# One chain step per unit, chain products on two banks, and retention folded into other bursts, in a two-layer hybrid decoder trunk

## The chip, the cores and the metric

The kernel runs on one core of one Trainium2 chip. The metric is the device time of one execution, in microseconds (us). The kernel before takes 576.5 us, the median of three runs (576.31 to 576.83).

## The reference

Two layers work on x, 512 tokens of width 1024, in float32. Each layer normalises x, projects it with one 1024 x 3904 matrix, sends the columns to four groups of width 256 (four heads of 64), multiplies each group's result by its SiLU gate, and adds the output projection of all four to x. Cut to what this change touches:

```python
def hybrid_layer(x, norm_w, w_in, w_out, ...):
    h = rmsnorm(x, norm_w)
    proj = h @ w_in
    p_rwkv, p_conv, p_moba, p_ret = jnp.split(proj, [...], axis=-1)
    y_rwkv = rwkv7_time_mix(p_rwkv[..., :RWKV_IN], ...) * jax.nn.silu(p_rwkv[..., RWKV_IN:])
    y_conv = short_conv_mix(p_conv[..., :3 * G], conv_w) * jax.nn.silu(p_conv[..., 3 * G:])
    y_moba = moba_attention(q, k, v, rel_bias) * jax.nn.silu(p_moba[..., 3 * G:])
    y_ret = retention_chunkwise(q, k, v) * jax.nn.silu(p_ret[..., 3 * G:])
    return x + jnp.concatenate([y_rwkv, y_conv, y_moba, y_ret], axis=-1) @ w_out

# rwkv7_time_mix, one step of the scan over tokens (then a layer norm per head)
state = (state * w_t[:, :, None, :] - s_kk[..., None] * (kk_t * a_t)[:, :, None, :]
         + v_t[..., None] * k_t[:, :, None, :])
y_t = jnp.einsum('bhij,bhj->bhi', state, r_t)

# retention_chunkwise, one step of the scan over chunks of 128 tokens
inner = jnp.einsum('bhnd,bhmd->bhnm', qc, kc) * decay_intra
y = jnp.einsum('bhnm,bhmd->bhnd', inner, vc) + jnp.einsum('bhnd,bhde->bhne', qc * q_decay, R)
R = R * chunk_decay + jnp.einsum('bhmd,bhme->bhde', kc * k_decay, vc)
# and after the scan: y = y * lax.rsqrt(mean(y * y) + NORM_EPS) per head
```

## The kernel before

**The stream of projections.** The large products are split in two parts each (`act_hi`, `act_lo`, `w_hi`, `w_lo`), and each of eight blocks of the inner dimension takes three matmuls of 128x512: one tile of the projection is 24 of them, in lines L772 to L775. The function `quarter` issues a quarter of a tile, 6 matmuls. A tile goes to PSUM bank 0 or 1 in turn. ScalarE makes `w_hi` (`tile_high`, L1295), GpSimd makes `w_lo` (L706), and ScalarE or VectorE takes the finished tile out of its bank (`copy`, L1403; the sigmoid or tanh of a gate, L1369; `conv_h`, L1479).

**The order.** Nothing is scheduled at run time. `layer_steps()` (L147 to L205) writes one list of steps, and every engine walks the same list and does its own part of each step. In the second half of a layer the list is built from 16 last tiles, retention's gates, attention's q and k, attention's gates, then the convolution's c, h, b and gates. Each tile has two slots of two quarters. `mid[i]` is what stands between the two quarters of slot i, `after[i]` what stands behind slot i: short bursts of small matmuls, and steps of ScalarE and VectorE only. An engine that has to wait in one step does not take the next.

**What hangs in the slots.**
- RWKV works on 8 chunks of 64 tokens: `inverse_x`, `inverse_y`, `corner_x`, `corner_t` build triangular inverses (they read `t_back`, data that went out to DRAM and come back transposed), `chunk_b` and `chunk_uw` the factors, `chunk_gh` what each chunk does to the state, then six steps `chain` 1 to 6 carry the state from chunk to chunk: TensorE (L1111 to L1124) multiplies, VectorE (L1938) scales, adds and stores the next state. `chunk_h`, `chunk_q`, `chunk_y1` and `chunk_y` make the outputs, `ln_square`, `ln_var`, `ln_recip` (L2009), `ln_scale` (L2014 on VectorE, L1541 on ScalarE) and `rwkv_finish` (L2018, L1867) the layer norm and the gate.
- Retention: `retain_scores`, `retain_state`, `retain_sum`, `retain_inner`, `retain_past`, `retain_out`, then its norm: `ret_low`, `ret_stat` (means on TensorE L885, added on VectorE L1984, L1987), `ret_root` (two square roots on ScalarE, L1560), `ret_recip` 0 to 3 (L1995), `ret_finish` 0 and 1 (L2002, L1867).
- Attention: six units (the loop over `u`), each `attend_scores` (TensorE L1008; VectorE adds the bias and takes the maximum, L1844, L1849; ScalarE the exponentials, L1464), `attend_norm` (L1856, L1859), `attend_turn` (transposes on TensorE L1019; ScalarE copies them out, L1470) and `attend_values` (L1035).

**Banks.** PSUM has eight banks. `bank_jobs()` (L225 to L320) lists for each job its bank and how many readers it has, in the order of the steps. `begin(job)` on TensorE waits until the previous user of that bank has been read by all its readers. Every chain step uses bank 7, and its four products of 64x64 stand side by side in it.

**The end of a layer.** The gate of the last tiles, `split_y` for each eighth of the concatenated y (ScalarE `act_hi`, L1572; VectorE `act_lo`, L2023) in the order `Y_ORDER`, and `out` 0 to 4, the output projection, which takes its blocks in that order.

## Time and profile before

| | |
|---|---|
| profiled execution, device time | 576.78 us |
| its span, first to last instruction | 575.0 us |
| TensorE matmul busy | 567.4 us, 99% of the span |
| VectorE, ScalarE, GpSimd busy | 381.0, 278.3, 249.3 us |
| mean granted TensorE clock | 0.997 |
| DMA, share of 16 engines' time, hardware queue | 39.4% |
| longest DMA groups: issue to landing | 3 to 8 us |

The span is 1.8 us shorter than the device time of the same execution; the profiled execution is 0.3 us above the median of the three runs. The first row of the table's engines is to be read with care: matmuls are pipelined, a 128x512 matmul is shown as 0.39 us long while the next starts 0.23 us after it, so "busy" says that TensorE had work in hand, not that every matmul came as early as it could. The granted clock is 0.9 of full speed or more in each fortieth of the span but the last (0.8).

### The profile page before, as it was taken

To read this page: it belongs to the slowest core of one execution; us is meant where nothing else is said; L and a number is where in the kernel's file an instruction comes from. 1 tells how busy PE (TensorE), PEld (TensorE's weight loads), DVE (VectorE), ACT (ScalarE), POOL (GpSimd) and SP (SyncE) were. 2 spreads that over 40 slices of the span, in tenths; PEclk is the share of its full clock that TensorE was granted. 3 is DMA by queue.
4 is the path that set the end of the run, shared out by engine and by line. 5 is a ranking of instruction groups with operands and counts; after the bars stand their busy time and mean duration, and the time that the engine had idled before them with its cause. 6 is when DMAs were issued, how large, how long until landed. Compare 5 with 4: busy or idle time off the path is not lost. (4 is left out here: it accounts for less than half of the span.)

```text
span 575.0 us, 12739 instructions
## 1 busy us (share of the span) xinstructions
PE 567.4 (99%) x5244; PEld 464.0 (81%) x5244; DVE 381.0 (66%) x644; ACT 278.3 (48%) x555; POOL 249.3 (43%) x197
## 2 busy tenths in 40 slices
PE   9999999999999999999999999999999999999995
PEld 7978888888877777888898788888888777788884
DVE  4999976482488557774543897947537865778163
ACT  5486231343574475534656743324357335735253
POOL 4946552044941323536335455402386313145340
PEclk9999999999999999999999999999999999999998
DMA  9546634056432122353535423332743321224513
GB/s 281 161 130 206 212 97 111 8 130 149 109 79 75 39 75 62 113 171 132 165 117 139 111 77 108 88 70 58 161 127 83 77 73 39 73 75 147 184 40 143
DMA packets 103373, 64.58 MB, mean 112 GB/s; under 512 B 29151, under 2 KB 94227, under 8 KB 103316
## 3 DMA queue, kind: packets, MB, share of 16 engines
q1 hardware_dynamic: 103316, 63.77, 39.4%
q8 instruction: 42, 0.69, 0.5%
q14 instruction: 15, 0.12, 0.1%
HBM read 55.61 MB, written 8.14 MB: 111 GB/s over the span
## 5 line engine op out<-in xcount | busy, mean ns | idle before, releaser
L706 POOL TENSOR_TENSOR w_lo<-w_raw,w_hi 128x512 fp32r<-128x512 f32 x156 | 216.6, 1409 | 283.0 <-ACT w_hi L1295 277.7
L772 PE MATMUL bank<-act_hi,w_hi 128*128 128x512 f32 x432 | 173.2, 401 | 0.0
L775 PE MATMUL bank<-act_lo,w_hi 128*128 128x512 f32 x432 | 168.5, 390 | 0.0
L774 PE MATMUL bank<-act_hi,w_lo 128*128 128x512 f32 x416 | 162.3, 390 | 0.0
L1295 ACT ACTIVATE w_hi<-w_raw 128x512 fp32r<-128x512 f32 x140 | 80.3, 622 | 74.1 <-PE bank L857 28.2
L772 PEld LDWEIGHTS bank<-act_hi,w_hi 128*128 128x128 f32 x432 | 81.1, 188 | 24.7 <-issue 8.2
L775 PEld LDWEIGHTS bank<-act_lo,w_hi 128*128 128x128 f32 x432 | 81.1, 188 | 17.4
L774 PEld LDWEIGHTS bank<-act_hi,w_lo 128*128 128x128 f32 x416 | 78.2, 188 | 14.8
L1221 PE MATMUL bank<-w_hi,act_hi 128*128 128x512 f32 x128 | 50.0, 390 | 0.0
L1223 PE MATMUL bank<-w_hi,act_lo 128*128 128x512 f32 x128 | 49.8, 389 | 0.0
L1222 PE MATMUL bank<-w_lo,act_hi 128*128 128x512 f32 x128 | 49.8, 389 | 0.0
L2028 DVE TENSOR_TENSOR x_or_y<-x_or_y,bank 128x512 f32<-128x512 f32 x16 | 11.0, 688 | 37.7 <-PE bank L1223 37.7
L1223 PEld LDWEIGHTS bank<-w_hi,act_lo 128*128 128x128 f32 x128 | 24.0, 188 | 5.1
L1222 PEld LDWEIGHTS bank<-w_lo,act_hi 128*128 128x128 f32 x128 | 24.0, 188 | 4.9
L1221 PEld LDWEIGHTS bank<-w_hi,act_hi 128*128 128x128 f32 x128 | 24.0, 188 | 4.9
L1464 ACT ACTIVATE pages<-pages,small 128x128 f32<-128x128 f32 (+3 forms) x32 | 17.9, 561 | 19.0 <-DVE small L1849 19.0
L855 PE MATMUL bank<-w_hi,act_hi 128*128 128x512 f32 x64 | 25.5, 398 | 0.0
L857 PE MATMUL bank<-w_hi,act_lo 128*128 128x512 f32 x64 | 25.0, 390 | 0.0
L856 PE MATMUL bank<-w_lo,act_hi 128*128 128x512 f32 x64 | 24.9, 390 | 0.0
L1369 ACT ACTIVATE x_or_y<-bank 128x512 f32<-128x512 f32 x16 | 9.6, 599 | 30.1 <-PE bank L775 30.1
L1470 ACT ACTIVATE pages<-bank 128x384 f32<-128x384 f32 (+1 forms) x24 | 11.4, 527 | 26.4 <-PE bank L1019 26.3
L1403 ACT ACTIVATE pages<-bank 128x512 f32<-128x512 f32 x16 | 9.6, 600 | 28.5 <-PE bank L775 28.5
(217 smaller groups left out, 961.0 us busy)
## 6 DMA issues: line engine op xcount, KB each, us to landing
w_raw<-in_w_in_dram SPq DMA_DIRECT2D x62, 512.0 KB, 4.1
w_raw<-in_w_out_dram SPq DMA_DIRECT2D x16, 512.0 KB, 3.8
pages<-in_x_dram SPq DMA_DIRECT2D x4, 512.0 KB, 6.3
x_or_y<-in_x_dram SPq DMA_DIRECT2D x4, 512.0 KB, 4.2
x_scratch<-x_or_y SPq DMA_DIRECT2D x4, 512.0 KB, 2.9
x_or_y<-x_scratch SPq DMA_DIRECT2D x4, 512.0 KB, 3.7
out_dram<-pages SPq DMA_DIRECT2D x8, 256.0 KB, 2.2
bias_scratch<-pages SPq DMA_DIRECT2D x1, 1280.0 KB, 8.1
```

The source lines that it names most:

```text
L706: ins = pool.tensor_tensor(low, raw, w_hi[:, i % HI, k, 0:n].bitcast(F32), ALU.subtract)
L772: mm(b[:, :], hi, act_hi[:, k, :], start=n == 0, stop=False)
L774: mm(b[:, :], lo, act_hi[:, k, :], start=False, stop=False)
L775: ins = mm(b[:, :], hi, act_lo[:, k, :], start=False, stop=n == KT - 1)
L855: mm(o, act_hi[:, n, tc], w_hi[:, :, n, :], start=n == 0, stop=False)
L856: mm(o, act_hi[:, n, tc], w_lo[:, :, n, :], start=False, stop=False)
L857: ins = mm(o, act_lo[:, n, tc], w_hi[:, :, n, :], start=False, stop=n == KT - 1)
L1221: mm(b[:, :], act_hi[:, k, tc], hi[:, wc], start=first, stop=False)
L1222: mm(b[:, :], act_hi[:, k, tc], lo[:, wc], start=False, stop=False)
L1223: ins = mm(b[:, :], act_lo[:, k, tc], hi[:, wc], start=False, stop=last)
L1295: go(w_hi[:, i % HI, k, 0:n], w_raw[:, i % RAW, k, 0:n], ACT.Copy).then_inc(s("w_high"), 1)
L1464: go(pb, pb, ACT.Exp, bias=row_max[:, n:n + 1], accum_out=row_sum[:, n:n + 1]).then_inc(s("prob"), 1)
```

## The change

- **Prologue.** The seven idle matmuls before the first projection become one, and VectorE waits for the norm weights' banks where it first reads them.
- **Retention.** `retain_scores` moves forward, behind RWKV's `scores` 2 and 3, into banks 2 and 3; `rotate rk1` and `wide 0 0` go ahead of those two steps. `retain_state` joins `chunk_b` in `after[1]`, `retain_inner` joins `inverse_x`, `retain_past` and `retain_out` 0 join `corner_x`, `retain_out` 1 `corner_t`. `ret_low`, `ret_stat`, `ret_root` and the first `ret_recip` come one to two slots later.
- **Chain.** Each attention unit u carries one chain step u+1 in `after[12+2u]`; before, steps stood in every slot or second slot from 13 on. All of attention moves one slot later. A chain step now writes two banks: 7, and the bank of the tile before the one that has just been computed (`1 - place_of[...]`). Its four products lie in four different 64x64 quarters of the array (the "quarter tiles"). VectorE stores the state with three instructions instead of two, and copies the first state and the chunk-end decays with three instead of one.
- **Layer norm.** `chunk_y1` comes in two halves, `chunk_y` moves from `after[19]` to `after[24]`, `ln_square` from `mid[21]` to `mid[25]`, `ln_var` from `mid[22]` to `after[26]`, and the four `ln_recip` from slots 22 to 26 to slots 26 to 28.
- **Output.** `Y_ORDER` ends 2, 3, 0, 1 instead of 0, 1, 2, 3 (0 and 1 are RWKV's eighths), and both `rwkv_finish` come later.

The diff, with parts left out:

```diff
@@ -147,8 +147,8 @@
...
-          ("copy", "rk0"), ("rotate", "rq1"), ("scores", 0), ("scores", 1), ("copy", "rk1"), ("rotate", "rk0"), ("to_rows", "v"), ("scores", 2),
-          ("scores", 3), ("wide", 0, 0), ("wide", 0, 1), ("rotate", "rk1"), ("wide", 0, 2), ("wide", 0, 3),
+          ("copy", "rk0"), ("rotate", "rq1"), ("scores", 0), ("scores", 1), ("copy", "rk1"), ("rotate", "rk0"), ("to_rows", "v"), ("rotate", "rk1"), ("wide", 0, 0), ("scores", 2),
+          ("scores", 3), ("retain_scores",), ("wide", 0, 1), ("wide", 0, 2), ("wide", 0, 3),
...
@@ -159,40 +159,39 @@
...
-    after[0] += [("retain_state",), ("retain_scores",)]
-    after[1] += [("retain_sum",), ("inverse_eye",)]
-    after[2] += [("retain_inner",), ("chunk_b",)]
...
-                    (INV0 + 2, ("corner_x",)), (INV0 + 3, ("corner_t",)), (9, ("ret_stat",)), (10, ("chunk_uw",)),
-                    (11, ("chunk_gh",)), (17, ("chunk_y1",)), (21, ("ln_square",)), (22, ("ln_var",))]:
...
+    after[1] += [("retain_state",), ("chunk_b",), ("inverse_eye",)]
+    after[2] += [("retain_sum",)]
+    after[9] += [("ret_low",)]
+    mid[10] += [("ret_stat",)]
+    for i, step in [(INV0, ("inverse_x",)), (INV0, ("retain_inner",)),
+                    (INV0 + 1, ("inverse_y",)), (INV0 + 1, ("inverse_yt",)),
+                    (INV0 + 2, ("corner_x",)), (INV0 + 2, ("retain_past",)), (INV0 + 2, ("retain_out", 0)),
+                    (INV0 + 3, ("corner_t",)), (INV0 + 3, ("retain_out", 1)), (10, ("chunk_uw",)),
...
-    after[9] += [("ret_root",), ("ret_recip", 0)]
+    after[10] += [("ret_root",), ("ret_recip", 0)]
...
-            mid[11 + 2 * u].append(("attend_turn", u - 1))
-            after[11 + 2 * u].append(("attend_values", u - 1))
...
-        if u in (1, 2, 3):
-            after[11 + 2 * u].append(("chain", 2 * u))
+                after[12 + 2 * u].append(("attend_out", u // 3 - 1))
         if u < UNITS:
-            (after[11 + 2 * u] if u else mid[10]).append(("attend_scores", u))
-            (mid[12 + 2 * u] if u else after[11]).append(("attend_norm", u))
-    mid[15][1:1] = [("chunk_q",), ("queries",)]
...
+            after[12 + 2 * u].append(("chain", u + 1))
+            (after[12 + 2 * u] if u else mid[11]).append(("attend_scores", u))
+            (mid[13 + 2 * u] if u else after[11]).append(("attend_norm", u))
+    after[12].append(("chunk_h",))
+    after[14].append(("chunk_q",))
+    mid[15].append(("queries",))
+    after[16].append(("chunk_y1", 0))
...
+    after[24].append(("chunk_y",))
+    after[26].append(("ln_var",))
+    for i, step in [(12, ("ret_recip", 1)), (16, ("ret_recip", 2)), (18, ("ret_recip", 3)), (19, ("ret_finish", 0)), (20, ("ret_finish", 1)),
+                    (21, ("conv_taps", 0)), (24, ("conv_taps", 1)), (26, ("ln_recip", 0)), (26, ("ln_recip", 1)), (27, ("ln_recip", 2)), (28, ("ln_recip", 3)),
+                    (27, ("ln_scale", 0)), (28, ("ln_scale", 1))]:
         after[i].append(step)
...
-    s += [("split_y", k) for k in Y_ORDER[:4]] + [("rwkv_finish", 1), ("split_y", 0), last[-1], ("conv_out", 0), ("split_y", 1), ("conv_out", 1)]
+    s += [("split_y", k) for k in Y_ORDER[:4]] + [("rwkv_finish", 0), last[-1], ("conv_out", 0), ("conv_out", 1), ("split_y", 2), ("split_y", 3), ("rwkv_finish", 1)]
...
-Y_ORDER = [6, 7, 4, 5, 0, 1, 2, 3]
-ROW_ORDER = [3, 2, 0, 1]
+Y_ORDER = [6, 7, 4, 5, 2, 3, 0, 1]
+ROW_ORDER = [3, 2, 1, 0]
...
         elif kind == "chain":
-            layer.append((f"chain{step[1]}", 7, 1))
+            layer += [(f"chain{step[1]}_0", 7, 1), (f"chain{step[1]}_1", 1 - place_of[projections[-1]], 1)]
         elif kind == "retain_scores":
-            layer += [("rs0", 5, 1), ("rs1", 6, 1)]
+            layer += [("rs0", 2, 1), ("rs1", 3, 1)]
...
-            idle(3)
             pe.wait_ge(s("const_a"), 16)
             turn(0, 0)
             turn(1, 0)
-            idle(4)
+            idle(1)
...
+                    banks = [begin(f"chain{c}_{p}", layer) for p in range(2)]
                     for p in range(2):
                         for hh in range(2):
-                            r = slice(64 * hh, 64 * hh + 64)
-                            ins = mm(b[r, p * N:(p + 1) * N], GT[r, p, c, :], ST[r, p, c, :], start=True, stop=True)
-                    end(ins, f"chain{c}", layer)
+                            r = head_rows(hh)
+                            ins = mm(banks[p][head_rows(hh ^ p), 0:N], GT[r, p, c, :], ST[r, p, c, :], start=True, stop=True)
+                        end(ins, f"chain{c}_{p}", layer)
...
-                        mark(dve.tensor_copy(w_end[:].rearrange("p a c -> p (a c)").unsqueeze(2), flat[:, :, CH:CH + 1]))
+                        mark(dve.tensor_copy(w_end[:, 0, :].unsqueeze(2), flat[:, 0:NCH, CH:CH + 1]))
+                        for hh in range(2):
+                            mark(dve.tensor_copy(w_end[head_rows(1 - hh), 1, :].unsqueeze(2), flat[head_rows(hh), NCH:2 * NCH, CH:CH + 1]))
...
-                    dve.tensor_copy(ST[:, :, 1, :], HP[:, :, 0, :]).then_inc(s("first_state"), 1)
+                    dve.tensor_copy(ST[:, 0, 1, :], HP[:, 0, 0, :]).then_inc(s("first_state"), 1)
+                    for hh in range(2):
+                        dve.tensor_copy(ST[head_rows(hh), 1, 1, :], HP[head_rows(1 - hh), 1, 0, :]).then_inc(s("first_state"), 1)
...
+                    b = [ps(f"chain{c}_{p}", layer) for p in range(2)]
+                    stt(ST[:, 0, c + 1, :], b[0][:, 0:N], w_end[:, 0, c:c + 1], HP[:, 0, c, :], ALU.mult, ALU.add).then_inc(done(f"chain{c}_0", layer), 1)
+                    for hh in range(2):
+                        o = head_rows(1 - hh)
+                        ins = stt(ST[head_rows(hh), 1, c + 1, :], b[1][o, 0:N], w_end[o, 1, c:c + 1], HP[o, 1, c, :], ALU.mult, ALU.add)
+                    ins.then_inc(done(f"chain{c}_1", layer), 1)
```

ScalarE's order around the exponentials of unit 0 and the copy of the tile `mk1` (the last row), in the first layer, before (L1560 is `ret_root`, L1498 `chunk_uw`, L1295 `tile_high`, L1464 the exponentials, L1403 the copy):

```order
L1560 ACTIVATE pages<-pages 128x512 [waits bank3_read]
L1498 ACTIVATE pages<-bank 128x512 [waits bank7_full]
L1498 ACTIVATE pages<-bank 128x512 [waits bank5_full]
L1498 ACTIVATE pages<-bank 128x512 [waits bank6_full]
L1498 ACTIVATE pages<-bank 128x512 [waits bank4_full]
L1295 ACTIVATE w_hi<-w_raw 128x512 [waits w_loaded1,bank0_full] x2
L1464 ACT_TABLE_LOAD
L1464 ACTIVATE pages,small<-pages,small 128x128 [waits logit_max]
L1464 ACTIVATE pages,small<-pages,small 128x256 [waits logit_max]
L1464 ACTIVATE pages,small<-pages,small 128x128 [waits logit_max]
L1464 ACTIVATE pages,small<-pages,small 128x256 [waits logit_max]
L1403 ACTIVATE pages<-bank 128x512 [waits bank1_full]
```

and now (the same functions stand two lines further down):

```order
L1500 ACTIVATE pages<-bank 128x512 [waits bank4_full]
L1297 ACTIVATE w_hi<-w_raw 128x512 [waits w_loaded1,bank0_full] x2
L1562 ACT_TABLE_LOAD
L1562 ACTIVATE pages<-pages 128x512 [waits bank2_read]
L1562 ACTIVATE pages<-pages 128x512 [waits bank3_read]
L1466 ACT_TABLE_LOAD
L1466 ACTIVATE pages,small<-pages,small 128x128 [waits logit_max]
L1466 ACTIVATE pages,small<-pages,small 128x256 [waits logit_max]
L1466 ACTIVATE pages,small<-pages,small 128x128 [waits logit_max]
L1466 ACTIVATE pages,small<-pages,small 128x256 [waits logit_max]
L1405 ACTIVATE pages<-bank 128x512 [waits bank1_full]
```

The square roots and their table load stood ahead of the four copies of `chunk_uw`; now they stand behind them and behind `tile_high`, next to the exponentials. The copy of `mk1` follows the exponentials in both.

VectorE's order at the same place, from the first `ret_recip` on, before (L1995 `ret_recip`, L1844 and L1849 `attend_scores` 0, L1911, L1904 and L1916 `chunk_gh`):

```order
L1995 RECIPROCAL pages<-pages 128x256 [waits ret_root]
L1844 SCALAR_TENSOR_TENSOR pages<-bank,bias 128x128 [waits bank2_full,bias_back]
L1844 SCALAR_TENSOR_TENSOR pages<-bank,bias 128x256
L1849 TENSOR_REDUCE small<-pages 128x1 [waits bank2_read]
L1849 TENSOR_REDUCE small<-pages 128x1
L1844 SCALAR_TENSOR_TENSOR pages<-bank,bias 128x128 [waits bank3_full]
L1844 SCALAR_TENSOR_TENSOR pages<-bank,bias 128x256
L1849 TENSOR_REDUCE small<-pages 128x1 [waits bank3_read]
L1849 TENSOR_REDUCE small<-pages 128x1
L1995 RECIPROCAL pages<-pages 128x256 [waits ret_root]
L1911 TENSOR_TENSOR pages<-bank,constants 128x4x64 [waits bank5_full]
L1911 TENSOR_TENSOR pages<-bank,constants 128x4x64
```

and now:

```order
L2004 RECIPROCAL pages<-pages 128x256 [waits ret_root]
L1915 TENSOR_TENSOR pages<-bank,constants 128x4x64 [waits bank5_full]
L1915 TENSOR_TENSOR pages<-bank,constants 128x4x64
L1915 TENSOR_TENSOR pages<-bank,constants 128x4x64 [waits bank6_full]
L1915 TENSOR_TENSOR pages<-bank,constants 128x4x64
L1908 TENSOR_TENSOR pages<-bank,chunk_decay 128x64 [waits bank7_full]
L1908 TENSOR_TENSOR pages<-bank,chunk_decay 128x64
L1908 TENSOR_TENSOR pages<-bank,chunk_decay 128x64 [waits bank4_full]
L1908 TENSOR_TENSOR pages<-bank,chunk_decay 128x64
L1920 COPY pages<-pages 128x64 [waits bank4_read,bank7_read]
L1922 COPY pages<-pages 64x64 x2
L1848 SCALAR_TENSOR_TENSOR pages<-bank,bias 128x128 [waits bank2_full,bias_back]
```

Unit 0's scores, which `logit_max` waits for, stood directly behind the first reciprocal; now `chunk_gh` with eleven instructions stands between.

VectorE's order at the end of the layer, before (L2009 `ln_recip`, L1888 `conv_b`, L2014 `ln_scale`, L2018 and L1867 `rwkv_finish`, L1777 a gate, L2023 `split_y`):

```order
L2009 RECIPROCAL pages<-pages 128x256 [waits bank7_read]
L1884 SCALAR_TENSOR_TENSOR pages<-pages,params 128x512 [waits conv_tap]
L1884 SCALAR_TENSOR_TENSOR pages<-pages,params 128x512 [waits dve_step]
L1888 TENSOR_TENSOR pages<-pages,bank 128x512 [waits bank0_full,dve_step]
L2009 RECIPROCAL pages<-pages 128x256 [waits bank5_read] x2
L2014 TENSOR_TENSOR pages<-pages 128x512 [waits dve_step]
L1888 TENSOR_TENSOR pages<-pages,bank 128x512 [waits bank1_full]
L2014 TENSOR_TENSOR pages<-pages 128x512 [waits dve_step]
L2018 TENSOR_TENSOR pages<-pages 128x512 [waits ln_affine]
L1867 SCALAR_TENSOR_TENSOR x_or_y<-pages,x_or_y 128x512 [waits dve_step]
L1777 SCALAR_TENSOR_TENSOR x_or_y<-x_or_y,bank 128x512 [waits bank0_read]
L2023 TENSOR_TENSOR act_lo<-x_or_y,act_hi 128x512 [waits y_hi] x4
```

and now:

```order
L1892 TENSOR_TENSOR pages<-pages,bank 128x512 [waits bank0_full]
L2018 RECIPROCAL pages<-pages 128x256 [waits bank7_read] x2
L1892 TENSOR_TENSOR pages<-pages,bank 128x512 [waits bank1_full]
L2018 RECIPROCAL pages<-pages 128x256 [waits bank5_read]
L2023 TENSOR_TENSOR pages<-pages 128x512 [waits dve_step]
L2018 RECIPROCAL pages<-pages 128x256 [waits bank5_read]
L2023 TENSOR_TENSOR pages<-pages 128x512 [waits dve_step]
L1781 SCALAR_TENSOR_TENSOR x_or_y<-x_or_y,bank 128x512 [waits bank0_read]
L2032 TENSOR_TENSOR act_lo<-x_or_y,act_hi 128x512 [waits y_hi] x4
```

All four reciprocals now stand behind the first `conv_b`, two of them behind the second or directly ahead of it, and `rwkv_finish` 0 has gone from ahead of the gate and the first splits to behind them.

## Rows read from the trace of the kernel before

**Rows 1.** Waits of TensorE over the span: us in total, times, longest.

```profile
PE bank L740 <- POOL pages L680: 1.0, 1, 1.0
PE bank L1035 <- ACT pages L1470: 0.3, 2, 0.2
PE bank L1047 <- issue: 0.2, 1, 0.2
```

**Rows 2.** Timeline of TensorE, slots 10 and 11 of layer 0: start, duration, line.

```profile
159.18 1.98 PE L1063 MATMUL bank<-pages 64*64 64x128 f32 x64
160.98 0.83 PE L1008 MATMUL bank<-pages 64*64 64x128 f32 x16
161.74 0.50 PE L772 MATMUL bank<-act_hi,w_hi 128*128 128x512 f32 x1
...
164.68 1.16 PE L1099 MATMUL bank<-pages 64*64 64x64 f32 x64
...
166.34 0.50 PE L772 MATMUL bank<-act_hi,w_hi 128*128 128x512 f32 x1
```

**Rows 3.** Timeline of ScalarE, the same slots.

```profile
159.84 1.15 ACT L1560 ACTIVATE pages<-pages 128x512 f32<-128x512 f32 x2
160.90 2.04 ACT L1498 ACTIVATE pages<-bank 128x512 f32<-128x512 f32 x4
162.81 1.17 ACT L1295 ACTIVATE w_hi<-w_raw 128x512 fp32r<-128x512 f32 x2
...
166.58 0.49 ACT L1464 ACTIVATE pages<-pages,small 128x256 f32<-128x256 f32 x1
...
168.05 0.60 ACT L1403 ACTIVATE pages<-bank 128x512 f32<-128x512 f32 x1 [0.89 <-PE bank L775]
```

**Rows 4.** Timeline of VectorE, the same slots.

```profile
160.50 1.75 DVE L1995 RECIPROCAL pages<-pages 128x256 f32<-128x256 f32 x1 [1.71 <-ACT pages L1560]
162.17 0.56 DVE L1844 SCALAR_TENSOR_TENSOR pages<-bank,bias 128x128 f32<-128x128 f32 x2
...
164.47 1.74 DVE L1995 RECIPROCAL pages<-pages 128x256 f32<-128x256 f32 x1
166.13 1.35 DVE L1911 TENSOR_TENSOR pages<-bank,constants 128x256 f32<-128x256 f32 x4
167.40 0.61 DVE L1904 TENSOR_TENSOR pages<-bank,chunk_decay 128x64 f32<-128x64 f32 x4
```

**Rows 5.** Timeline of VectorE, unit 2: its first score and last norm.

```profile
178.14 0.56 DVE L1844 SCALAR_TENSOR_TENSOR pages<-bank,bias 128x384 f32<-128x384 f32 x1 [0.15 <-PE bank L1008]
...
182.30 0.42 DVE L1859 TENSOR_SCALAR pages<-pages,small 128x384 f32<-128x384 f32 x1
```

**Rows 6.** Timeline of VectorE, norms of unit 0, two pairs.

```profile
168.44 0.55 DVE L1859 TENSOR_SCALAR pages<-pages,small 128x128 f32<-128x128 f32 x2
...
169.10 1.64 DVE L1859 TENSOR_SCALAR pages<-pages,small 128x128 f32<-128x128 f32 x2
```

**Rows 7.** Timeline of GpSimd, the same microseconds.

```profile
169.31 2.59 POOL L706 TENSOR_TENSOR w_lo<-w_raw,w_hi 128x512 fp32r<-128x512 f32 x2 [3.19 <-ACT w_hi L1295]
```

**Rows 8.** Timeline of ScalarE, end of layer 0.

```profile
238.35 1.28 ACT L1369 ACT_TABLE_LOAD   x1
241.63 0.60 ACT L1369 ACTIVATE x_or_y<-bank 128x512 f32<-128x512 f32 x1 [1.99 <-PE bank L775]
```

**Rows 9.** Timeline of VectorE, end of layer 0.

```profile
236.80 0.69 DVE L2014 TENSOR_TENSOR pages<-pages 128x512 f32<-128x512 f32 x1
...
243.82 3.82 DVE L2023 TENSOR_TENSOR act_lo<-x_or_y,act_hi 128x512 fp32r<-128x512 f32 x4 [0.87 <-ACT act_hi L1572]
```

**Rows 10.** Timeline of TensorE, `inverse_x` of layer 0.

```profile
138.29 1.16 PE L944 MATMUL bank<-pages 64*64 64x64 f32 x64
```

**Rows 11.** Timeline of SyncE's queue, the loads of `t_back`, layer 0.

```profile
129.37 2.66 SPq L526 DMA_DIRECT2D pages<-t_scratch  x4
```

**Rows 12.** Timeline of TensorE, the idle matmuls ahead of the first projection.

```profile
11.56 1.25 PE L740 MATMUL bank<-pages 128*128 128x128 f32 x8
```

54 lines of the change are left out of this document (23 added, 31 removed).

## Prediction

> A difference below 0.2% (1.2 us) can't be told from no change in this kernel. I forecast **585.5 us**, 1.6% slower.
>
> **What bounds the kernel now.** I read the shares first: TensorE has work in hand for 99% of the span. Then its waits: beside one microsecond at the very start, the whole execution holds 0.3 us behind the copies of turned probabilities and 0.2 us without a cause that the profile shows [rows 1]. So every microsecond counts that TensorE's stream gains or loses, and the other engines count only where they make it wait. Then I read the timelines of slots 10 to 12 side by side, since the change packs reciprocals, chunk results, scores and the first chain step there [rows 2 to 4]. In them the 12 matmuls between two bursts take 164.68 - 161.74 = 2.94 us, where 12 in an undisturbed run take 12 x 0.227 = 2.72 [rows 2]. Last the end of the layer [rows 8, 9]: the tanh of the second-last gate at 241.63 waits for its tile, not for the norm; the tile of the last gate follows it, 24 x 0.227 = 5.4 us, so `out` 0 starts about E = 246.9.
>
> **The main term: chain step 1 waits for a bank.** Times here count from the start of `chunk_uw`.
> TensorE now runs `chunk_uw` (160.98 - 159.18 = 1.8), 12 matmuls (2.9), `chunk_gh` (166.34 - 164.68 = 1.7) with unit 0's scores (161.74 - 160.98 = 0.8), 18 matmuls (one and a half times 2.94, less a slow start: 4.3), and stands before chain 1 at 11.5 [rows 2]. That step writes bank 7 and the bank of `mk1`, so it waits until ScalarE has copied `mk1`.
> That copy stands behind the four exponentials of unit 0. ScalarE: the copies of `chunk_uw` end near 3.1, one after the last product is there (2.04 long from 1.0), `tile_high` 1.17 -> 4.2, table load 1.28 [rows 8] -> 5.5, square roots 1.15 for both, the first at 6.1 [rows 3]. VectorE: reciprocal 1.75 less the overlap of neighbours -> 7.8; four additions of `chunk_gh` 1.35 -> 9.1; decays 0.61 -> 9.7; three small copies, where there was one, about 0.5 (an estimate from the decays, 0.15 each) -> 10.2; scores and maxima of unit 0 as between 162.17 and 164.47, 2.3 -> 12.5 [rows 4]. ScalarE: the last exponential 0.49 and its read-out -> 13.2, the copy 0.60 -> 13.9 [rows 3]. The wait is 13.9 - 11.5 = 2.4 us a layer. Now that row at 168.05 waits 0.89 for its own tile, and nothing waits for it.
> Bounds: if every operation of VectorE overlaps as well as its neighbours there, 1.8; if its adds meet GpSimd's halves (below), 3.4. I take 2.4, for both layers 4.8.
>
> **Turn 4 waits for its norm.** VectorE has, behind unit 4's scores, the second `ret_finish`, a chain step of three instructions and then the reciprocals and norms. The nearest case, unit 2, has the first score at 178.14 and the last norm ending at 182.72 [rows 5], with `ret_finish` between: 4.6 us. TensorE comes after 18 matmuls, 4.3. That alone makes 0.3. What is added is GpSimd. A pair of norms takes 0.55 us, the next pair 1.64: it starts at 169.10, GpSimd's subtraction at 169.31, and the pair ends at 170.74, just after the first of the two (half of 2.59) [rows 6, 7]. ScalarE makes `w_hi` behind a tile's end, and GpSimd starts 0.8 us later, which is where unit 4's norm falls. I take 1.2; bounds 0.25 (norm clear of GpSimd) and 2.2 (both norms caught). Turns 2 and 3 have no `ret_finish` ahead and pass by about 0.2 us: 0.1 together. Two layers: 2.6.
> The Trainium skill, "SBUF — State Buffer", on engine ports, describes this as an exclusive lock between VectorE and GpSimd that is held for the full instruction; the trace agrees with its 1.64 against 0.55.
>
> **Values 4 and 5.** Before the copies of the turned probabilities ScalarE now has the copy of a `conv_h` tile, which waits for VectorE. Such a copy is 0.6 long [rows 3]; those waits are the 0.3 in two places now [rows 1]. I take 0.35 for each unit, 0.7 a layer, between 0 and 1.2; two layers 1.4.
>
> **`out` 0 waits for the splits.** `ln_var` has moved from `mid[22]` to `after[26]`, 5 slots before E: 5 x 2.7 and the run-in behind bursts, E - 14.5. Its burst and the square roots (1.15 for two [rows 3]) end at E - 13.1. VectorE then has, in this order, two reciprocals (1.7 each: E - 9.8), `conv_b` 1 (0.6), the third reciprocal (E - 7.4), `ln_scale` 0 (0.6), the fourth (E - 5.0), `ln_scale` 1 (E - 4.3). ScalarE scales behind that (0.8: E - 3.5), loads the tanh table (1.28 [rows 8]: E - 2.2) and only then does the tanh of gate 0. From that tanh to the first four splits' first end is 3.1 us now: tanh at 241.63, first split at 243.82 and 0.9 of its 3.82 for four [rows 8, 9]. So E - 2.15 + 3.1 = E + 0.95, where TensorE is ready at E. Now it is E - 2.1. I take 1.0; bounds 0 and 2.0 (an `ln_recip` or split caught by GpSimd). Two layers 2.0. `rwkv_finish` 0 no longer stands ahead of the gate on VectorE; without that move the wait would be longer by its two instructions.
>
> **What TensorE gains.** By the list, the second half of a layer has 21 separate bursts instead of 22: `retain_scores` rides in an existing stretch, and `retain_state` joins `chunk_b`. A burst less saves the slow start (2.94 against 12 x 0.227 = 2.72) and the drain behind its last record, 0.35. The count of small matmuls stays. With the few tenths of smoother runs and today's waits [rows 1] I take 0.7 a layer, between 0.2 and 1.2; two layers -1.4. The four products of a chain step in four quarters change nothing in my sum: by `inverse_x`'s 64 records in 1.16 us [rows 10] the eight records of a step take 0.15, 0.3 with a drain.
> The Trainium skill, "TensorEngine Tiling (Array Packing)", Key Properties, says that different tiles load and multiply in parallel. If that halved each step, the gain would be at most 0.15 x 12 = 1.8 and the time 583.7; no row here shows it, and I don't count it.
>
> **Once only.** `inverse_x` comes 2.9 us earlier than its 138.29 [rows 10], at 135.4: the four loads of `t_back` are issued until 129.37 + 2.66 = 132.0 and need some 3.4 more to land [rows 11], 135.4. Level: I take +0.3, bounds 0 and 0.8. The wait of `chunk_b` without a cause [rows 1] may go or move: -0.2. The idle matmuls ahead of the first projection take 1.0 of 1.25 us for four [rows 12]; three fewer are 0.75, of which the splits of the weights let about half through: -0.4, with bounds -0.75 and +1.0, since the clock granted there may rise later if TensorE did less before.
> Hidden: the two more copies of `w_end` (0.1 us on VectorE, with two microseconds to spare), a third instruction in each chain step, and `scores` 2 and 3 a little later.
>
> **Sum.** 4.8 + 2.6 + 1.4 + 2.0 - 1.4 + 0.3 - 0.2 - 0.4 = +9.1 us. On the profiled execution (576.8) that makes 585.9, on the median (576.5) 585.6. With all lower bounds: 3.6 + 0.5 + 0 + 0 - 2.4 - 0.2 - 0.75 = +0.8; with all upper ones over 15. Neither is likely, since the terms are independent.
>
> **Rivals.**
> - *TensorE's own work stays the bound* (the other side). Decisive is whether `mk1` is copied before 11.5: if exponentials or scores start 2.4 us earlier than I add up (the square roots done right behind the first copies of `chunk_uw`, or `chunk_gh` much shorter in its new place), the bank is free. With norms clear of GpSimd only the gains stay: -1.4 -0.6 = 574.5. For it: TensorE waits almost nowhere now. Against: ScalarE's list fixes the order, and each duration is a row.
> - *Only the bank's wait.* Chain 1 waits, but turn 4, the values and `out` are covered within tenths: 4.8 + 2 x 0.3 (turn 4 without GpSimd) - 1.4 - 0.3 = +3.7, 580.2. For it: those three margins are each below 1 us of my own adding up.
> - *GpSimd catches more.* Turns 2 and 3, 0.2 us from the edge, lose 1.2 each as well (4.8 over both layers; half of it, if one in two is caught, 2.4), and the prologue costs 1.0 instead of giving 0.4: 9.1 + 2.4 + 1.4 = +12.9, 589.4. For it: with all norms in the same place behind a tile's end, what happens in one unit happens in all.
>
> **Chances.** My forecast 0.5, only the bank 0.2, GpSimd more 0.2, TensorE's own work 0.1. The range from 578.5 to 591 leaves out the last rival and half a tenth above. Faster by over 0.2%: 0.09; within 0.2%: 0.05 (lower bounds throughout); slower: 0.86. The forecast's own range is 583 to 588.
>
> **What would show it.** In the profile after: a wait of TensorE at the chain's line in unit 0, ended by ScalarE's copy, 2 to 3 us, once in each layer; a wait at the turn of unit 4 ended by VectorE, with a norm over 0.8 us long beside GpSimd; a wait at the first matmul of `out` ended by the splits; no wait at `chunk_b`. If the copy of `mk1` ends before TensorE reaches the chain, the main term is wrong; if TensorE's waits sum to less than 3 us and the time is still above 580, the cost is in the stream itself.

## The result and the profile after

The changed kernel takes 600.2 us (median of four runs, 598.9 to 601.1) against 576.6 of the kernel before: ratio 1.041 (95% interval 1.038 to 1.043), 23.6 us slower. The forecast was 585.5 with a range up to 591. The direction was right; the loss was 2.6 times the forecast one (23.6 us for 9.1).

The profiled execution took 598.87 us with a span of 597.1, 22.1 us more than before. First the shares of the page:

```profile
PE 570.4 (96%) x5232; PEld 463.6 (78%) x5232; DVE 384.2 (64%) x664; ACT 277.5 (46%) x555; POOL 246.5 (41%) x197
```

TensorE's share fell from 99% to 96%, and its busy time still grew by 3.0 us, though it multiplies the same things. The waits of TensorE over the span (total, times, longest) answer to [rows 1]:

```profile
PE bank L1018 <- DVE pages L1863: 8.3, 6, 2.1
PE bank L1123 <- ACT pages L1405: 5.4, 2, 2.7
PE bank L1223 <- issue: 1.6, 2, 0.8
PE bank L1223 <- POOL w_lo L706: 1.5, 2, 0.8
PE bank L1034 <- ACT pages L1472: 1.2, 4, 0.4
PE bank L740 <- POOL pages L680: 1.0, 1, 1.0
PE bank L979 <- issue: 0.7, 1, 0.7
PE bank L734 <- DVE pages L1655: 0.5, 1, 0.5
PE bank L817 <- DVE act_lo L1645: 0.2, 1, 0.2
PE bank L817 <- POOL w_lo L706: 0.2, 1, 0.2
```

They add to 20.6 us where they were 1.5. So 19.1 of the 22.1 us are waits, and 3.0 lie outside them. Each is looked for in a timeline below.

**Chain step 1.** The place of [rows 2 to 4], now. TensorE (start, duration, operation; in brackets the wait and what ended it):

```profile
158.11 1.98 PE L1062 MATMUL bank<-pages 64*64 64x128 f32 x64
...
172.39 0.49 PE L1123 MATMUL bank<-pages 64*64 64x64 f32 x8 [2.69 <-ACT pages L1405]
172.63 0.48 PE L1102 MATMUL bank<-pages 64*64 64x64 f32 x6
...
175.58 0.50 PE L771 MATMUL bank<-act_hi,w_hi 128*128 128x512 f32 x1
```

ScalarE:

```profile
163.65 1.15 ACT L1562 ACTIVATE pages<-pages 128x512 f32<-128x512 f32 x2
...
169.61 0.40 ACT L1466 ACTIVATE pages<-pages,small 128x128 f32<-128x128 f32 x1 [3.50 <-DVE small L1853]
...
171.67 0.57 ACT L1405 ACTIVATE pages<-bank 128x512 f32<-128x512 f32 x1
```

VectorE:

```profile
164.31 1.75 DVE L2004 RECIPROCAL pages<-pages 128x256 f32<-128x256 f32 x1 [3.88 <-ACT pages L1562]
165.99 1.35 DVE L1915 TENSOR_TENSOR pages<-bank,constants 128x256 f32<-128x256 f32 x4
...
168.63 0.62 DVE L1848 SCALAR_TENSOR_TENSOR pages<-bank,bias 128x128 f32<-128x128 f32 x2
```

The step starts 14.3 us after the start of `chunk_uw` at 158.11, where the forecast had 13.9, and TensorE had been ready at 11.6 (forecast 11.5). ScalarE's order is what was forecast: square roots at 163.65 behind `tile_high`, exponentials from 169.61, the copy of `mk1` (L1405) at 171.67. The wait is 2.69 us; 2.4 was forecast.

Behind it stands what no term of the forecast held. Windows of three microseconds in the same trace (busy of each engine, then the granted TensorE clock, the DMA share and GB/s): ahead of the wait, behind it, and behind a later wait of 2.06 us:

```profile
166.00:169.00 3.00, 3.00 (x15) 2.46 (x14) 2.80 (x14) 0.10 (x1) 0.00 (x0) 1.00 0.59 166
172.40:175.40 3.00, 3.00 (x104) 3.00 (x104) 1.00 (x4) 0.89 (x2) 2.49 (x2) 0.50 0.00 0
211.00:214.00 3.00, 3.00 (x37) 2.09 (x36) 1.04 (x2) 0.49 (x1) 0.00 (x0) 1.00 0.66 174
```

The granted clock is 0.50 behind the chain's wait, 1.2 GHz instead of 2.4; the low stretch is 3.4 us long and begins in the last tenths of the wait. In it runs `chunk_h`, 96 short records: from 172.63 to the next full matmul at 175.58 is 2.95 us. In a1_bank4 (below), where this place runs at full clock, the same stretch takes 172.54 - 170.78 = 1.76. That is 1.2 us, and 1.0 in layer 1 (2.78 us). With the chain step itself it is 2.3 us for both layers: from chain step 1 to step 2 it is 10.33 and 10.18 us here, and 9.11 in each layer of a1.

**Unit 3 and unit 4.** VectorE around the norms (L1863) of unit 3 and unit 4:

```profile
205.79 1.74 DVE L2004 RECIPROCAL pages<-pages 128x256 f32<-128x256 f32 x1
...
207.59 0.55 DVE L1863 TENSOR_SCALAR pages<-pages,small 128x128 f32<-128x128 f32 x2
...
208.25 2.50 DVE L1863 TENSOR_SCALAR pages<-pages,small 128x128 f32<-128x128 f32 x2
...
217.05 0.68 DVE L2011 TENSOR_TENSOR pages<-pages 128x512 f32<-128x512 f32 x1
...
218.56 1.45 DVE L1863 TENSOR_SCALAR pages<-pages,small 128x384 f32<-128x384 f32 x1
...
220.13 1.23 DVE L1863 TENSOR_SCALAR pages<-pages,small 128x384 f32<-128x384 f32 x1
```

GpSimd in the same microseconds:

```profile
208.12 2.49 POOL L706 TENSOR_TENSOR w_lo<-w_raw,w_hi 128x512 fp32r<-128x512 f32 x2 [7.01 <-ACT w_hi L1297]
218.54 2.60 POOL L706 TENSOR_TENSOR w_lo<-w_raw,w_hi 128x512 fp32r<-128x512 f32 x2 [7.93 <-ACT w_hi L1297]
```

Between unit 3's scores and its norms stands `ret_recip` 3, the 1.74 us at 205.79. The first pair of norms takes 0.55 us; the second starts inside GpSimd's subtraction and takes 2.50. TensorE's turn of unit 3 waits 2.06 us for it. In unit 4 it is `ret_finish` 1 (L2011 and the line behind it, 1.3 us) that comes ahead of the norms, and both are caught: 1.45 and 1.23 us where 0.42 was [rows 5]. TensorE waits 1.29 and 0.79 us. Both layers show the same to a hundredth, which makes 8.3 us. The turns cost somewhat more than these waits: from chain step 4 to step 6, where both turns lie, it is 22.64 us in each layer, and 17.77 in a2_recip (below), which has none of the three waits. That is 9.7 us for both layers.

Unit 2 has a reciprocal ahead of its norms as well (`ret_recip` 2, 1.74 us at 195.84). There the last norm starts at 198.23 and GpSimd's subtraction at 198.28; the norm takes 0.49 us, and TensorE does not wait. So turn 2 passed by a few hundredths: the reciprocal costs time only where it pushes a norm into a subtraction.

**The output projection.** TensorE's two waits in it, in layer 0:

```profile
255.82 0.47 PE L1223 MATMUL bank<-w_hi,act_hi 128*128 128x512 f32 x1 [0.78 <-issue]
...
286.70 0.50 PE L1223 MATMUL bank<-w_hi,act_hi 128*128 128x512 f32 x1 [0.68 <-POOL w_lo L706]
```

The first, at its start, is the splits of the first y blocks (the profile names no releaser); 1.0 was forecast, 0.8 came. The second, 31 us later, waits for a `w_lo` of the output weights. No step of the forecast had it. SyncE's queue shows where it comes from (start, time to issue):

```profile
257.44 11.09 SPq L526 DMA_DIRECT2D x_or_y<-in_x_dram  x4
268.57 11.20 SPq L548 DMA_DIRECT2D w_raw<-in_w_out_dram  x4
```

The last of the four loads of x waits until the last y block is split (VectorE ends it at 268.17), and the next four weight tiles stand behind them in the queue: they start 268.57 - 255.82 = 12.8 us after the output projection does. In the kernel before, the same loads began 8.6 us after it, at 255.44, with the projection starting at 246.87, and the last split had ended at 255.04.

### The profile page after: what moved, and what is told of

The parts are those of the page before. It is cut to its first block, busy times and chain, and to the rows that moved or that the text cites. A ratio compares the mean times of both kernels' runs of the same rounds, so it can differ in the third digit from the quotient of the medians.

```text
span 597.1 us, 12755 instructions
## 1 busy us (share of the span) xinstructions
PE 570.4 (96%) x5232; PEld 463.6 (78%) x5232; DVE 384.2 (64%) x664; ACT 277.5 (46%) x555; POOL 246.5 (41%) x197
## 4 chain that ended last, share of the span: by engine, by line
PE 68%; DVE 15%; ACT 5%; DMA 4%; issue 3%; POOL 3%; SPq 0%; POOLq 0%; ACTq 0%; DVEq 0%
PE bank L771 13%; PE bank L774 13%; PE bank L773 12%; DMA w_raw<-in_w_out_dram 3%; POOL w_lo L706 3%; PE bank L854 3%; PE bank L856 2%; PE bank L855 2%; DVE act_lo L2032 2%; DVE pages L2018 2%; PE bank L1034 2%; PE bank L1223 2%; DVE pages L1848 2%; PE bank L1225 2%; PE bank L1224 2%
## 5 line engine op out<-in xcount | busy, mean ns | idle before, releaser
L706 POOL TENSOR_TENSOR w_lo<-w_raw,w_hi 128x512 fp32r<-128x512 f32 x156 | 213.9, 1391 | 304.1 <-ACT w_hi L1297 302.6
L773 PE MATMUL bank<-act_hi,w_lo 128*128 128x512 f32 x416 | 162.2, 390 | 0.0
L773 PEld LDWEIGHTS bank<-act_hi,w_lo 128*128 128x128 f32 x416 | 78.2, 188 | 15.0
L701 POOL TENSOR_TENSOR w_hi<-w_raw,units 128x512 fp32r<-128x512 f32 (+1 forms) x20 | 20.9, 1043 | 9.9 <-DMA w_raw<-in_w_in_dram 5.9
L1711 DVE TENSOR_TENSOR stat_lo<-pages,stat_hi 128x512 fp32r<-128x512 f32 x16 | 14.6, 933 | 14.7 <-ACT pages L1533 11.4
```

The source lines that it names most:

```text
L701: pool.tensor_tensor(w_hi[:, i % HI, k, 0:n], raw, one.unsqueeze(2).to_broadcast([P, H, n]), ALU.mult).then_inc(s("w_high_pool"), 1)
L706: ins = pool.tensor_tensor(low, raw, w_hi[:, i % HI, k, 0:n].bitcast(F32), ALU.subtract)
L773: mm(b[:, :], lo, act_hi[:, k, :], start=False, stop=False)
```

## The experiments

Thirteen kernels ran, in four groups; each group ran beside the kernel before on one chip (whose median was 576.5 to 577.0). Differences of about 1 us are read from the ratios.

**a1_bank4: the chain's second bank.**

```diff
-  (f"chain{step[1]}_1", 1 - place_of[projections[-1]], 1)
+  (f"chain{step[1]}_1", 4 if step[1] == 1 else 1 - place_of[projections[-1]], 1)
```

> The changed kernel with one bank moved: the second product pair of chain step 1 goes to bank 4 (free since first_state) instead of the bank of mk1. Theory W (each wait of TensorE is lost time, and the 2.7 us wait also halves the granted clock for 3.3 us behind it, in which chunk_h's 96 records take 2.95 instead of 1.65 us): both the wait (2 x 2.7) and the slow stretch (2 x 1.4) go, 600.2 - 8.2 = 592.0. Rival M (the wait moves: the norm of unit 0 or chain 2 is next): at most a third of it comes back, 597 or more, with a new wait at the first turn. Rival N (wait without clock effect): 5.4 come back, 594.8, and chunk_h still takes about 2.9 us.

Measured: 593.1 us (592.3 to 593.8), ratio 1.028 (1.026 to 1.030), 7.1 us less. No wait at the chain is left, and the stretch behind it is at full clock, so the wait was the bank's alone. But the slow clock has moved:

```profile
209.50:212.50 3.00, 3.00 (x30) 1.67 (x28) 0.23 (x1) 0.00 (x0) 0.00 (x0) 0.51 0.45 134
```

The same wait of 2.06 us at unit 3's turn (it ends at 207.78 here) is now followed by the half clock, which in the changed kernel it was not. Theory W was right on the stretch behind the chain and wrong that nothing would take its place: the trace has two slow stretches, as many as the changed kernel's. So between the two profiled executions only the waits came back: the spans differ by 5.5 us, the waits by 5.8. How often the clock falls is not fixed even within one kernel. The mean granted clock of a1's four executions is 0.991, 0.996, 0.994 and 0.994, the first one being the trace, and a slow stretch of 3.4 us takes 0.003 off that mean. This is where the medians' 7.1 us can hold more than the traces' 5.5.

**a4_idle: work in place of the wait.** The output of the ten matmuls is read by nobody.

```diff
                         pe.wait_ge(*at("first_state", layer))
+                        for _ in range(10):
+                            mm(bank[4][:, 0:P], ident, ident, start=True, stop=True)
```

> The changed kernel with ten more matmuls of 128x128 on constants, into bank 4, whose output nobody reads, between the wait for first_state and the wait for the banks in chain step 1. They fill some 2.5 of the 2.7 us in which TensorE waits. If the idle time drops the granted clock: the clock stays at 2.4 GHz, chunk_h takes 1.65 us again, 600.2 - 2.8 = 597.4. If the clock falls for another reason (the 64x64 shapes, the other engines' load): no change, 600.2, and chunk_h at 2.9 us.

Measured: 598.2 us (596.9 to 599.0), ratio 1.037 (1.035 to 1.039), 2.0 us less. The matmuls run from 169.26, the step starts at 172.11, no later than without them:

```profile
169.26 2.39 PE L1117 MATMUL bank<-constants 128*128 128x128 f32 x20
172.11 0.34 PE L1125 MATMUL bank<-pages 64*64 64x64 f32 x8 [0.46 <-ACT pages L1407]
```

The stretch behind the step is at full clock, and the clock falls behind the next long wait instead:

```profile
172.20:175.20 3.00, 3.00 (x109) 2.76 (x110) 2.04 (x9) 0.81 (x2) 2.52 (x2) 1.00 0.03 5
210.30:213.30 3.00, 3.00 (x16) 1.84 (x15) 0.21 (x1) 0.02 (x1) 0.00 (x0) 0.50 0.63 168
```

So the short shapes alone do not lower the clock; with the idle time filled, this place stays at full clock in both layers. Between the profiled executions nothing was won: the spans are 597.0 and 597.1, and two slow stretches stand at unit 3 in place of the two at the chain. The medians' 2.0 us fit the other executions, two of which have a mean granted clock of 0.996 where the changed kernel's four have 0.990 to 0.993.

**a2_recip: two steps of VectorE.**

```diff
-  (18, ("ret_recip", 3)), (19, ("ret_finish", 0)), (20, ("ret_finish", 1)),
+  (17, ("ret_recip", 3)), (19, ("ret_finish", 0)), (19, ("ret_finish", 1)),
```

> The changed kernel with two steps of VectorE moved: ret_recip 3 from after[18] to after[17], ret_finish 1 from after[20] to after[19]. Theory W: the reciprocal between unit 3's scores and norms pushes the norms into GpSimd's subtraction (one pair takes 2.50 us), and ret_finish does so for unit 4 (1.45 and 1.23 us). Without them the norms end before GpSimd starts: waits of 2.06 and 1.29 + 0.79 go in each layer, -8.3, 591.9. Rival M: the norms stay slow since GpSimd's start follows the same tile end, and only the 1.7 and 1.4 us of the moved steps count where they are longer than the margin: -3 to -4, 596.5.

Measured: 588.8 us (588.4 to 590.4), ratio 1.022 (1.020 to 1.024), 11.4 us less. TensorE's waits at the turns fall from 8.3 to 0.3 us:

```profile
PE bank L1123 <- ACT pages L1405: 5.4, 2, 2.7
...
PE bank L1018 <- DVE pages L1863: 0.3, 2, 0.2
```

Two steps that had idle time of VectorE half a slot or a slot ahead of them cost almost half of the whole change. Theory W had the 8.3. Of the further 3 us, 1.5 are what the turns cost beside their waits (9.7 in all), and a part is the slow clock: in this trace it comes in layer 0 only, though the chain's wait of 2.7 us is there in both layers.

**c2_bank_recip: both.** Edit: the two above together, without the idle matmuls.

> The changed kernel with both edits that gave time back: bank 4 for chain step 1, and ret_recip 3 and ret_finish 1 one slot earlier. In the two kernels with one edit each the stretch at half clock was still there, behind the wait that was left (behind unit 3's turn, or behind chain step 1). Theory W (a wait of 2 us or more can drop the clock, and no such wait is left): no stretch below full clock before the tail, and the gains add to more than their sum: 600.2 - 7.1 - 11.4 = 581.7 by the sum, about 580 with the last stretch gone. Rival (the clock falls for some other reason): a half-clock stretch of 3.3 us is still there in each layer, 582 or more.

Measured: 582.5 us (580.9 to 583.0), ratio 1.011 (1.009 to 1.012), 17.6 us less than the changed kernel. There is no stretch below full clock before the tail, over 568 us:

```profile
2.00:570.00 568.00, 562.45 (x5217) 458.89 (x5216) 377.52 (x657) 272.67 (x547) 246.97 (x188) 1.00 0.40 112
```

The longest wait left, but for the first microsecond, is 0.8 us. The single gains are 18.5 together, so the two add to a little less than their sum, not more, and the expected 580 was not reached.

**a3_ln: the layer norm one slot earlier.**

```diff
-  after[24].append(("chunk_y",)); after[26].append(("ln_var",)); (25, ("ln_square",))
+  after[23].append(("chunk_y",)); after[25].append(("ln_var",)); (24, ("ln_square",))
```

with the four `ln_recip` and two `ln_scale` one slot earlier as well (lines put together here).

> The changed kernel with the layer norm one slot earlier: chunk_y after[23], ln_square mid[24], ln_var after[25], the reciprocals and scales one slot earlier each. Theory W: VectorE's and ScalarE's chain ends 2.7 us earlier, out 0 finds its splits (-0.8), the last splits end 1.9 us earlier, with them the loads of x and of the next weights of the output projection, and the second wait in out (0.7) shrinks to 0.1 or less: -1.4 a layer, 597.4. Rival: the earlier chunk_y waits for chain 6 or meets GpSimd, and the gain is below 1 us (599.2 or more). A rival on the second wait: it comes from the one load fewer that was issued ahead of the norm weights, not from the splits; then only 0.8 a layer comes back, 598.6.

Measured: 605.1 us (604.4 to 606.6), ratio 1.050 (1.048 to 1.052), 4.9 us slower than the changed kernel. The edit was badly placed. `ln_square` in `mid[24]` stands ahead of unit 5's turn, and ScalarE works its list in order:

```profile
231.40 1.20 ACT L1510 ACTIVATE pages<-bank 128x512 f32<-128x512 f32 x2
232.68 0.63 ACT L1551 ACTIVATE stat_hi<-pages 128x512 fp32r<-128x512 f32 x1
233.21 0.61 ACT L1552 ACTIVATE pages<-pages 128x512 f32<-128x512 f32 x1
...
234.89 1.08 ACT L1472 ACTIVATE pages<-bank 128x512 f32<-128x512 f32 x2
```

Six instructions of the output's copies and squares (L1510 to L1552, 3.5 us) go ahead of the copies of the turned probabilities (L1472), and TensorE waits 2.65 us for those in each layer, with the half clock behind (in this trace the chain's wait has it in layer 0 only). The wait at the output's start did halve, 0.8 to 0.4.

**c3_bank_recip_ln: the same, with `ln_square` in `after[24]`, on top of c2.**

> As c2_bank_recip, and the layer norm one slot earlier, with ln_square behind unit 5's values (after[24]) instead of ahead of its turn, where ScalarE's squares held up the copies of the turned probabilities for 2.7 us. Theory W: out 0 waits 0 instead of 0.8 and the second wait in out falls below 0.2 instead of 0.5 to 0.8, as VectorE's last splits come earlier: -2.5 against c2, 577.5. Rival (the second wait hangs on the order of loads): -1.6, 578.5.

Measured: 581.4 us (580.1 to 582.5), ratio 1.008 (1.007 to 1.010), 1.1 us less than c2, which the intervals do not separate. The start of the output waits 0.4 instead of 0.8, but the wait at `w_lo` is 0.9 in each layer, no smaller, and the weight loads start 12.8 us behind the output's start as in c2 and in the changed kernel. So a norm one slot earlier does not cure that one.

**c4_old_end: c3 with the old order at the end.**

```diff
-Y_ORDER = [6, 7, 4, 5, 2, 3, 0, 1]
+Y_ORDER = [6, 7, 4, 5, 0, 1, 2, 3]
-... + [("rwkv_finish", 0), last[-1], ("conv_out", 0), ("conv_out", 1), ("split_y", 2), ("split_y", 3), ("rwkv_finish", 1)]
+... + [("rwkv_finish", 1), ("split_y", 0), last[-1], ("conv_out", 0), ("split_y", 1), ("conv_out", 1)]
```

and `rwkv_finish` 0 back in `after[28]`, `ROW_ORDER` as before.

> As c3_bank_recip_ln, with the old order at the end (Y_ORDER, ROW_ORDER and the places of rwkv_finish as before). Theory E: the wait at w_lo (0.9 a layer) goes, since the last splits and the loads behind them come earlier; but rwkv_finish 0 stands ahead of the gate on VectorE again and lengthens the wait at out 0 from 0.4 to about 1.5: 581.4 - 1.8 + 2.2 = 581.8. Rival W: the w_lo wait stays and out 0 waits longer: 583.5.

Measured: 579.7 us (579.4 to 580.1), ratio 1.005 (1.003 to 1.006), 1.7 us less than c3 (1.9 by the ratios). The `w_lo` wait is gone, the weight loads start 11.1 us behind the output's start, and the start of the output waits no longer than in c3:

```profile
PE bank L1035 <- ACT pages L1473: 1.9, 4, 0.7
...
PE bank L1224 <- issue: 0.8, 2, 0.4
```

I had expected `rwkv_finish` 0 on the way to the gate to cost 1.1 us a layer there; it stands in time in which VectorE waited for ScalarE anyway.

**b6_end: the end's order alone, on the kernel before.** Edit: the reverse of the last one.

> The kernel before with the end's part of the change alone: the y blocks in the order 6, 7, 4, 5, 2, 3, 0, 1, rwkv_finish 0 behind the first four splits, rwkv_finish 1 and the splits of 0 and 1 last; the layer norm where it was. Theory E (the second wait in out, 0.7 us a layer, comes from this order: the last splits end 12.4 us after the output projection starts instead of 8.5, and the loads of x and of the next weights stand behind them on SyncE): a wait of 0.4 to 0.8 in each layer at a w_lo, +1.2, 577.7, and no wait at out 0. Rival W (it comes from the later layer norm alone): no new wait, 576.5.

Measured: ratio 1.000 (0.999 to 1.001), and no new wait. The order at the end costs nothing where the norm stands as in the kernel before: the first splits start 3.1 us ahead of the output there, in c3 only 1.0, and the weight loads 10.1 us behind its start. So c4 shows that the wait needs the new order, and b6 that the order alone does not bring it. That the late norm is the other half fits these times; it was not tried alone with the old order.

**b2_two_banks: the chain's two banks and quarters alone, on the kernel before.** Edit: the hunks of the diff on `chain`, `first_state` and `w_end`, and in `by_chunk` the place of "h"; every step stays in its slot.

> The kernel before with the chain's part of the change alone: two banks, four products in four 64x64 quarters, three instructions of VectorE to a step instead of two, three copies of the first state and of w_end; all steps in their old places. Theory W: the chain stands beside covered work on VectorE: between 0 and +0.6, 576.8. Rival Q (products in different quarters run side by side): 0.15 us less for each of 12 steps, 574.7. Rival V (VectorE's third instruction reaches the turns behind it): +0.3 us for each of 12 steps, 580.

Measured: 580.0 us (579.6 to 581.6), ratio 1.006 (1.005 to 1.007), 3.4 us slower. The expectations missed the reason:

```profile
PE bank L773 <- DVE pages L1948: 3.8, 6, 0.8
```

L773 is the first matmul of a new tile. Chain steps 2, 4 and 6 stood in the odd `after` there, between two tiles, and the bank they borrow is the one in which the next tile starts at once: it waits 0.8, 0.4 and 0.8 us for VectorE to read the product. In the changed kernel the steps stand in the even `after`, in the middle of a tile, and that wait does not exist. Two more waits, 0.6 and 0.4 us, are of the "issue" kind (below). The step itself did get shorter. The first chain step and the record behind it, in the kernel before:

```profile
172.04 0.45 PE L1123 MATMUL bank<-pages 64*64 64x64 f32 x8
172.33 0.33 PE L1103 MATMUL bank<-pages 64*64 64x64 f32 x6
```

and in b2:

```profile
173.39 0.34 PE L1125 MATMUL bank<-pages 64*64 64x64 f32 x8
173.56 0.33 PE L1104 MATMUL bank<-pages 64*64 64x64 f32 x6
```

The next record comes 0.28 or 0.29 us behind a step's first one before, and 0.16 or 0.17 in b2, in all twelve steps. That is 0.12 us a step, 1.4 in all, near Rival Q's 0.15; the new waits hide it in the time. The two banks and the four quarters came together, so the rows do not tell which of them it is.

**b1_retention and b5_ret_past: retention's part alone, on the kernel before.**

```diff
-  after[0] += [("retain_state",), ("retain_scores",)];  after[2] += [("retain_inner",), ("chunk_b",)]
+  after[1] += [("retain_state",), ("chunk_b",), ("inverse_eye",)]; after[2] += [("retain_sum",)]
   # both: retain_scores behind scores 3, retain_inner with inverse_x
   # b1:   retain_past, retain_out 0 with inverse_y (mid[6]), retain_out 1 mid[7], ret_low after[7], ret_stat mid[9]
   # b5:   retain_past, retain_out 0 with corner_x (mid[7]), retain_out 1 mid[8], ret_low after[8], ret_stat after[9]
```

> The kernel before with retention's part of the change alone: retain_scores behind scores 3 in banks 2 and 3, retain_state with chunk_b, retain_inner with inverse_x, retain_past and retain_out 0 with inverse_y, retain_out 1 with corner_x; the norm of retention stays where it was. Theory W: one burst fewer in each layer, 0.35 each, and the wait in chunk_b gone: -0.7 to -1.0, 575.6. Rival (inverse_x comes too early for its transposed data and waits, retain_out 1 too late for ret_low): +0.5 to +1.5, 577.5.

> As b1_retention (the kernel before with retention folded into other bursts), but retain_past and retain_out 0 stand with corner_x as in the changed kernel, and retention's means follow one half slot later, in after[9]. In b1 the only new waits were 0.98 and 1.41 us inside retain_past, which the profile puts down to nothing, where three bursts of 64 short matmuls follow each other (inverse_y, inverse_yt, retain_past). Theory F (a third burst in a row runs out of instructions): with two in a row there is no such wait, b1 - 2.4 = 576.0, and against before -0.5. Rival (retain_past waits for its data, which retain_sum makes late): the wait moves along or is gone by the later place, but the means then wait: 577 or more.

Measured: b1 578.4 us, ratio 1.003 (1.002 to 1.004), slower; b5 576.2 us, ratio 0.999 (0.998 to 1.000), a shade faster. In b1 TensorE stops inside `retain_past` (L1190), the third burst in a row:

```profile
141.36 1.16 PE L979 MATMUL bank<-x_or_y,pages 64*64 64x64 f32 x64
142.34 1.13 PE L990 MATMUL bank<-pages,x_or_y 64*64 64x64 f32 x64
143.27 0.43 PE L1190 MATMUL bank<-pages 64*64 64x64 f32 x8
144.68 1.03 PE L1190 MATMUL bank<-pages 64*64 64x64 f32 x48 [0.98 <-issue]
```

Eight records have run when it stops, so it does not wait for the burst's first data, and the profile names no releaser ("issue"). With two bursts in a row b5 has no such wait, nor any other but the first microsecond of the span. That fits TensorE running out of instructions, and the traces hold a sign of it. The profile has a DMA queue that it calls "instruction", which moves 42 blocks of 16 KB in each execution. b1's transfers from 142.1 to 142.4 us hold one, which starts at 142.21, 2.5 us ahead of the restart at 144.68:

```profile
q8 instruction: 1, 0.02, 24.4%
```

The fifteen traces, with those of the two kernels compared, hold 15 such stops apart from the waits at the output projection's start; each ends 2.3 to 3.1 us behind the start of such a block, and 1.3 to 1.7 us behind its end. I call the cause likely: the times agree in each case, and b5 takes the stop away, but no run changed the supply of instructions alone. The changed kernel had the same kind of wait once, 0.7 us in `inverse_y` (L979) of layer 1.

**b3_prologue and b7_ret_past_pro: the prologue's part alone, and with b5.** Edit: the hunks on `idle` and `nw`.

> The kernel before with the prologue's part of the change alone: one idle matmul instead of seven, and VectorE's later wait for the norm weights. In the changed kernel the first projections started 0.98 us earlier and 0.25 to 0.6 us of it was left 70 us later. Theory: 576.5 - 0.4 = 576.1. Rival (the start hangs on the split weights, or the clock rises later): 0 to +1.

> The kernel before with the two parts of the change that were no slower alone: b5_ret_past (ratio 0.9989) and b3_prologue (0.9988). If they add, ratio 0.9977, about 1.3 us below the kernel before, faster than both kernels. Rival (both gains end at the same limit, a w_lo or a load that is not ready earlier): 0.9989, no better than either.

Measured: b3 576.0 us, ratio 0.999 (0.998 to 1.000); b7 576.5 us, ratio 1.000 (0.999 to 1.001). The two small gains do not add in the time. In b7's trace they do until layer 1 (the output projection of layer 0 starts at 245.8, against 246.9 before), and then a wait of 0.7 us of the "issue" kind in `inverse_y` takes over half of it. No version was clearly better than the kernel before.

## Why the forecast was wrong

- **Chain step 1.** Mechanism and size right: 2.69 us for 2.4, with every instruction ahead of it within 0.5 us of its forecast place (a1 takes the wait away with one bank). What was missing is its price: the half clock behind it, 2.3 us for both layers. The forecast spoke of the clock in the prologue alone. In all traces the fall came only beside a wait of 2 us or more, and not each such wait brought it.
- **Turns.** This is the step that failed. "Turns 2 and 3 have no `ret_finish` ahead and pass by about 0.2 us" was wrong for turn 3: `ret_recip` 3, on the same line of the diff, stands between unit 3's scores and norms with 1.74 us. That makes 2 x 2.06. In turn 4 the upper bound came true (1.29 + 0.79 = 2.1, not 1.2), since both norms were caught by GpSimd. Together 8.3 us of waits, 9.7 with what goes with them, instead of 2.6, and a2 brings back 11.4. The nearest rival is "GpSimd catches more", which I gave 0.2. It had the norms caught, but not the reciprocal that pushes them there, and it added 2.4 us where 7.1 came. That turn 2 passed, as forecast, was luck: it too has a reciprocal ahead, and missed GpSimd by 0.05 us.
- **Values.** 1.2 us in all, for 1.4.
- **`out` 0.** 0.8 a layer for 1.0, by the mechanism forecast. The second wait, about 0.75 a layer, was not seen: I followed the first split and not the last one, behind which SyncE's loads stand. c4 shows that it needs the new order, b6 that it needs something beside it, probably the late norm.
- **TensorE's gains.** 1.4 and 0.4 (prologue) were forecast. In c2 the clock is full, the span 579.1 is 4.1 us above before, and the waits are 5.0 us above: some 0.9 came in that execution, the fastest of its four; by c2's median (582.5) nothing is left. The step from 0.29 to 0.17 us in the chain, which the sum put at nothing, is worth 1.4 alone, so what the sum did count (one burst fewer, smoother runs) gave nothing that shows. b5 and b3 put the two parts at 0.1% each, at the edge of what can be measured.
- **Once only.** `inverse_x` found its data (no wait there), `chunk_b`'s 0.2 went, and 0.7 of its kind came in `inverse_y`.

In sum, of the 22.1 us in the traces: 7.7 the chain's wait with the clock behind it (forecast 4.8), 9.7 the turns (2.6), 3.1 the output projection (2.0), 1.2 the values (1.4), 0.7 the stop in `inverse_y`, and 0.9 new waits in and behind the prologue (forecast -0.4). From this go the 0.5 of waits that the kernel before had and the 0.9 above, which leaves 21.9. c4, with the four causes mended, is still 0.5% slower than before; its waits hold 1.9 us at the values, 0.8 at the output's start, 0.8 of the "issue" kind in `inverse_y` and 1.0 in and behind the prologue. What the later slots of attention cost apart from these was not tried by itself.

## What to carry to other kernels

When a list is moved, write down for every wait on the path all that now stands ahead of its releaser on that engine, each entry of the edited line by name: one overlooked reciprocal of 1.7 us was the largest error here. Ask also what the pushed work will meet: the same reciprocal ahead of unit 2 cost nothing. Price a wait of two microseconds in dense TensorE work with the clock behind it, and follow the last reader of a buffer as well as the first, since the next loads queue behind the last. A PSUM bank borrowed for a short product is free only if neither its late reader ahead nor its next user behind is near.
